# Stick-breaking attention layer on one core: output projection on six PSUM banks, with the FFN norm's transposes, copies and first gate matmuls reordered

## The reference, cut to what matters

```python
def rmsnorm(x, g):
    return x * lax.rsqrt(jnp.mean(x * x, axis=-1, keepdims=True) + RMS_EPS) * g
...
hn = rmsnorm(x, ln_mix_pre[i])
mixed = stick_breaking_mixer(hn, sb_w_qkv[j], sb_w_o[j])   # ends in o @ w_o
x = x + rmsnorm(mixed, ln_mix_post[i])
hn = rmsnorm(x, ln_ffn_pre[i])
x = x + rmsnorm(swiglu_ffn(hn, ffn_w_gu[i], ffn_w_down[i]), ln_ffn_post[i])
```

## Time and profile before

| | us |
|---|---|
| three timed runs | 1458.83, 1458.40, 1454.26 (median 1458.4) |
| the profiled execution, its own time | 1454.86 |
| its span, from first to last instruction | 1453.1 |
| around the span | 1.76 |
| TensorE matmuls busy | 1381.3 (95%) |
| VectorE, ScalarE, GpSimd busy | 697.4, 533.7, 379.9 |
| mean granted TensorE clock | 0.98 of full |

### The profile page before, as it was taken

How to read it: one execution, slowest core, us unless ns; L and a number is a source line. 1 busy time by engine, 2 the same in 40 slices (tenths; PEclk the granted TensorE clock), 3 DMA queues, 4 the chain that set the end, 5 groups by cost and what they waited for, 6 DMA issues and landing times.

```text
span 1453.1 us, 18360 instructions
## 1 busy us (share of the span) xinstructions
PE 1381.3 (95%) x6848; PEld 1153.4 (79%) x6848; DVE 697.4 (48%) x850; ACT 533.7 (37%) x948; POOL 379.9 (26%) x244
## 2 busy tenths in 40 slices
PE   5999999999999986997899999999999999999995
PEld 4788888888888875786688888888888888888884
DVE  6578788787887888232312222313031322223138
ACT  5566666666666664233122111111212121111113
POOL 4111011011011033263053233232413232332326
PEclk9999999999999988998899999999999999999998
DMA  4000000000000013020011111110102111111102
GB/s 188 30 30 21 25 30 30 15 29 29 15 29 29 15 52 123 30 73 29 15 58 59 44 44 43 43 58 29 67 20 72 43 58 43 43 43 43 58 14 117
DMA packets 18336, 66.66 MB, mean 46 GB/s; under 512 B 2032, under 2 KB 2032, under 8 KB 18288
## 3 DMA queue, kind: packets, MB, share of 16 engines
q1 hardware_dynamic: 16560, 59.78, 11.8%
q10 hardware_dynamic: 1728, 6.29, 1.3%
HBM read 61.87 MB, written 4.19 MB: 45 GB/s over the span
## 4 chain that ended last, share of the span: by engine, by line
PE 91%; DVE 6%; ACT 1%; DMA 1%; POOL 0%; issue 0%; POOLq 0%; ACTq 0%; DVEq 0%
PE bank L1134 11%; PE bank L1133 11%; PE bank L1135 11%; PE bank L980 6%; PE bank L982 6%; PE bank L981 6%; PE bank L1181 5%; PE bank L1180 5%; PE bank L1182 5%; PE bank L1084 4%; PE bank L1059 2%; PE bank L1058 2%; PE bank L1056 2%; PE bank L1104 2%; PE bank L1103 2%; PE bank L1029 2%
## 5 line engine op out<-in xcount | busy, mean ns | idle before, releaser
L681 POOL TENSOR_TENSOR w_lo<-raw,w_hi 128x1024 fp32r<-128x1024 f32 x89 | 216.7, 2439 | 770.4 <-ACT w_hi L421 770.2
L1133 PE MATMUL bank<-hnT_hi,w_hi 128*128 128x512 f32 x704 | 277.3, 394 | 2.9 <-DVE hnT_lo L782 2.9
L1134 PE MATMUL bank<-hnT_lo,w_hi 128*128 128x512 f32 x704 | 278.5, 396 | 0.0
L1135 PE MATMUL bank<-hnT_hi,w_lo 128*128 128x512 f32 x704 | 276.0, 392 | 0.0
L421 ACT ACTIVATE w_hi<-raw 128x1024 fp32r<-128x1024 f32 x89 | 93.4, 1060 | 404.6 <-PE bank L1135 353.4
L913 DVE TENSOR_TENSOR sg<-bank,sg 128x512 f32<-128x512 f32 x44 | 30.4, 692 | 437.7 <-ACT sg L614 437.7
L856 DVE TENSOR_TENSOR_SCAN stay<-stay,diag_one 128x256 f32<-128x256 f32 (+7 forms) x128 | 196.2, 1533 | 3.8 <-ACT stay L541 3.8
L927 DVE TENSOR_TENSOR y<-bank,y 128x512 f32<-128x512 f32 x176 | 119.3, 690 | 94.4 <-PE bank L1182 93.1
L1133 PEld LDWEIGHTS bank<-hnT_hi,w_hi 128*128 128x128 f32 x704 | 132.8, 189 | 34.7 <-DVE hnT_lo L782 3.5
L1135 PEld LDWEIGHTS bank<-hnT_hi,w_lo 128*128 128x128 f32 x704 | 132.9, 189 | 29.9
L429 ACT ACTIVATE AT_hi<-bank 128x512 fp32r<-128x512 f32 (+1 forms) x160 | 89.0, 556 | 183.2 <-PE bank L1084 182.5
(11 more groups left out here) (100 smaller groups left out, 2134.4 us busy)
## 6 DMA issues: line engine op xcount, KB each, us to landing
raw<-in_units SPq DMA_DIRECT2D x98, 512.0 KB, 3.3
acc<-in_x SPq DMA_DIRECT2D x8, 512.0 KB, 8.7
x_in<-in_x ACTq DMA_DIRECT2D x8, 512.0 KB, 3.4
out<-y SPq DMA_DIRECT2D x7, 512.0 KB, 2.6
g_pre_s<-in_mix_pre ACTq DMA_DIRECT2D x1, 512.0 KB, 5.5
g_post_t<-in_mix_post ACTq DMA_DIRECT2D x1, 512.0 KB, 4.2
g_ffn_t<-in_ffn_pre ACTq DMA_DIRECT2D x1, 512.0 KB, 3.7
g_out<-in_ffn_post ACTq DMA_DIRECT2D x1, 512.0 KB, 3.7
```

The source lines that it names most:

```text
L681: nc.gpsimd.tensor_tensor(w_lo[slot], raw[:, raw_slot, :], w_hi[slot].bitcast(F32), ALU.subtract).then_inc(w_ready, 1)
L1133: nc.tensor.matmul(bank_ap, wh, hnT_hi[:, kt, cols], start=(kt == 0), stop=False)
L1134: nc.tensor.matmul(bank_ap, wh, hnT_lo[:, kt, cols], start=False, stop=False)
L1135: mm = nc.tensor.matmul(bank_ap, wl, hnT_hi[:, kt, cols], start=False, stop=(kt == KT - 1))
```

## The change

Six mixed banks instead of four (`OB` added). The wait for the FFN's gain gets a semaphore of its own and moves behind the first scaling. On ScalarE the high part of tile t + 2 is copied between the squares of the two halves; on VectorE its low part comes ahead of the scaling. Norm tiles 0 and 1 are transposed before the last projection tile, tiles 1 and 3 into `OB`; their copies come first after it. The first gate runs in two halves of 256 columns. The transposes 4, 5 and 6 with 7 stand behind the groups (0,0), (2,0) and (1,0), and on VectorE hn(4) and hn(5) are made before the last scaling, hn(6) behind it, hn(7) after the low parts of tile 6.

```diff
--- before.py
+++ after.py
@@ -304,14 +304,20 @@
 FIRST_ACC_B = ACCB + OB
 GATEB, UPB = ZB, OB
 YB = ACCB + TB
-MIXB = ACCB + ZB
-FIRST_GATE_B = [ZB[0], ACCB[0], ZB[1], ACCB[1]]
+MIXB = ACCB + ZB + OB
+FIRST_GATE_B = [ACCB[0], ZB[0], ACCB[1], ZB[1]]
 ...
+def norm_bank(n):
+    if n < T_TRANS:
+        return TB[n % 2]
+    return (OB if (n - T_TRANS) // 2 in (1, 3) else TB)[n % 2]
 ...
@@ -337,6 +343,7 @@
 raw_in = [sem("raw_in0"), sem("raw_in1")]
 gain_in = sem("gain_in")
 gain2_in = sem("gain2_in")
+gain_ffn_in = sem("gain_ffn_in")
 gain3_in = sem("gain3_in")
 x_again = [sem("x_again0"), sem("x_again1")]
 out_done = sem("out_done")
@@ -578,30 +585,51 @@
     split_at(0, [])
     step(PAIRS, 0, proj=False, slots=TAIL_SLOTS)
     act.wait_ge(av_done, Z_ALL)
-    act.dma_start(g_ffn_t[:, :], g_ffn_pre.partition_broadcast(P)).then_inc(gain2_in, 16)
-    for t in range(NT):
-        for c in range(2):
-            act.wait_ge(mix_full, 2 * t + c + 1)
-            act.wait_ge(sq_done, square_index("mix", t, c))
-            nc.scalar.activation(junk_t[:, 0:HALF], MIXB[(2 * t + c) % 4][:, :], ACT.Square,
-                                 accum_out=ss_mix[:, 2 * t + c:2 * t + c + 1]).then_inc(sq_done, 1)
-        if t + 2 < NT:
-            o_hi_copy(t + 2)
+    act.dma_start(g_ffn_t[:, :], g_ffn_pre.partition_broadcast(P)).then_inc(gain_ffn_in, 16)
+    def mix_square(t, c):
+        act.wait_ge(mix_full, 2 * t + c + 1)
+        act.wait_ge(sq_done, square_index("mix", t, c))
+        nc.scalar.activation(junk_t[:, 0:HALF], MIXB[(2 * t + c) % 6][:, :], ACT.Square,
+                             accum_out=ss_mix[:, 2 * t + c:2 * t + c + 1]).then_inc(sq_done, 1)
+    def x2_square(t):
         act.wait_ge(x2_ready, t + 1)
         if t + 2 < NT:
             act.dma_start(x_in[:, t % 2, :], x_tiles[:, t + 2, :]).then_inc(x_again[t % 2], 16)
         act.wait_ge(sq_done, square_index("x2", t))
         nc.scalar.activation(blocks(junk_t[:, :]), x2(t), ACT.Square,
                              accum_out=ss[:, 2 * NT + t:2 * NT + t + 1]).then_inc(sq_done, 1)
-        if t in (1, 2):
-            split_at(t, [(t_full, T_TRANS)])
-    for t in range(NT):
+    def norm_hi(t):
         for half in range(2):
             n = T_TRANS + 2 * t + half
             t_hi_copy(n, hnT_hi[:, 4 * half:4 * half + 4, t * P:(t + 1) * P],
-                      TB[n % 2][:, :].rearrange("p (k c) -> p k c", k=4))
+                      norm_bank(n)[:, :].rearrange("p (k c) -> p k c", k=4))
+    for t in range(NT - 1):
+        mix_square(t, 0)
+        if t + 2 < NT:
+            o_hi_copy(t + 2)
+        mix_square(t, 1)
+        x2_square(t)
+        if t in (1, 2):
+            split_at(t, [(t_full, T_TRANS)])
+    act.wait_ge(mix_full, 2 * NT)
+    norm_hi(0)
+    norm_hi(1)
+    for c in range(2):
+        mix_square(NT - 1, c)
+    for t in (2, 3, 4):
+        norm_hi(t)
+    x2_square(NT - 1)
+    for t in (5, 6, 7):
+        norm_hi(t)
     act.dma_start(g_out[:, :], g_ffn_post.partition_broadcast(P)).then_inc(gain3_in, 16)
     def ffn_chunk(g, e, par, c):
@@ -783,7 +811,7 @@
     def norm_lo(index, t, half):
         ks, cols = slice(4 * half, 4 * half + 4), slice(t * P, (t + 1) * P)
-        t_lo_sub(index, hnT_lo[:, ks, cols], TB[index % 2][:, :].rearrange("p (k c) -> p k c", k=4),
+        t_lo_sub(index, hnT_lo[:, ks, cols], norm_bank(index)[:, :].rearrange("p (k c) -> p k c", k=4),
                  hnT_hi[:, ks, cols])
@@ -880,31 +908,39 @@
                                        in1=blocks(g_ffn_t[:, :]), op0=ALU.mult,
                                        op1=ALU.mult).then_inc(hn_ready, 1)
-    dve.wait_ge(gain2_in, 32)
-    for t in range(NT):
+    dve.wait_ge(gain2_in, 16)
+    def mix_scale(t):
         dve.wait_ge(rstd_done, NT + 2 * t + 1)
         for c in range(2):
-            nc.vector.scalar_tensor_tensor(out=x2(t, c), in0=blocks(MIXB[(2 * t + c) % 4][:, :]),
+            nc.vector.scalar_tensor_tensor(out=x2(t, c), in0=blocks(MIXB[(2 * t + c) % 6][:, :]),
                                            scalar=rstd[:, NT + t:NT + t + 1],
                                            in1=blocks(g_post_t[:, c * HALF:(c + 1) * HALF]),
                                            op0=ALU.mult, op1=ALU.mult).then_inc(mix_scaled, 1)
+    def norm_tile(t):
+        for half in range(2):
+            norm_lo(T_TRANS + 2 * t + half, t, half)
+    for t in range(NT - 1):
         if t + 2 < NT:
             o_lo_sub(t + 2)
+        mix_scale(t)
+        if t == 0:
+            dve.wait_ge(gain_ffn_in, 16)
         if t < RING:
             hn(t)
-    def norm_tile(t):
-        for half in range(2):
-            norm_lo(T_TRANS + 2 * t + half, t, half)
-    for t in range(RING):
+    hn(4)
+    hn(5)
+    for t in range(4):
         norm_tile(t)
-    for t in range(RING, NT, 2):
-        hn(t)
-        hn(t + 1)
+    mix_scale(NT - 1)
+    hn(6)
+    for t in (4, 5, 6):
         norm_tile(t)
-        norm_tile(t + 1)
+    hn(7)
+    norm_tile(7)
     def ffn_chunk(g, e, par, c):
         n = 4 * g + 2 * e + c
@@ -1021,9 +1057,9 @@
         if c == 0 and j == 0:
             pe.wait_ge(o_lo, t + 1)
-        if j == 0 and 2 * t + c >= 4:
-            pe.wait_ge(mix_scaled, 2 * t + c - 3)
-        dst = MIXB[(2 * t + c) % 4][:, :]
+        if j == 0 and 2 * t + c >= 6:
+            pe.wait_ge(mix_scaled, 2 * t + c - 5)
+        dst = MIXB[(2 * t + c) % 6][:, :]
         cols = slice(c * HALF, (c + 1) * HALF)
         oh, ol = o_hi_t[:, t % 2, j, :], o_lo_t[:, t % 2, j, :]
         nc.tensor.matmul(dst, oh, hnT_hi[:, j, cols], start=(j == 0), stop=False)
@@ -1119,20 +1155,31 @@
     step(PAIRS - 1, 1, proj=False)
     step(PAIRS, 0, proj=False, slots=TAIL_SLOTS)
-    for t in range(2, NT):
+    def out_project(t):
         for c in range(2):
             for j in range(PAIRS):
                 wo_part(t, c, j)
-    def gate_up(is_up, c, slot, bank_ap):
-        cols = slice(c * HALF, (c + 1) * HALF)
-        for kt in range(KT):
-            wh = w_hi[slot][:, kt * P:(kt + 1) * P]
-            wl = w_lo[slot][:, kt * P:(kt + 1) * P]
-            nc.tensor.matmul(bank_ap, wh, hnT_hi[:, kt, cols], start=(kt == 0), stop=False)
-            nc.tensor.matmul(bank_ap, wh, hnT_lo[:, kt, cols], start=False, stop=False)
-            mm = nc.tensor.matmul(bank_ap, wl, hnT_hi[:, kt, cols], start=False, stop=(kt == KT - 1))
+    def gate_up(is_up, c, slot, bank_ap, halves=1):
+        w = HALF // halves
+        for b in range(halves):
+            if halves > 1:
+                pe.wait_ge(t_lo, T_TRANS + 4 * (b + 1))
+            cols = slice(c * HALF + b * w, c * HALF + (b + 1) * w)
+            dst = bank_ap[:, b * w:(b + 1) * w]
+            for kt in range(KT):
+                wh = w_hi[slot][:, kt * P:(kt + 1) * P]
+                wl = w_lo[slot][:, kt * P:(kt + 1) * P]
+                last = b == halves - 1 and kt == KT - 1
+                nc.tensor.matmul(dst, wh, hnT_hi[:, kt, cols], start=(kt == 0 and b == 0), stop=False,
+                                 skip_group_check=halves > 1)
+                nc.tensor.matmul(dst, wh, hnT_lo[:, kt, cols], start=False, stop=False,
+                                 skip_group_check=halves > 1)
+                mm = nc.tensor.matmul(dst, wl, hnT_hi[:, kt, cols], start=False, stop=last,
+                                      skip_group_check=halves > 1)
         mm.then_inc(up_full if is_up else gate_full, 1)
     def gate_up_first(m, c):
@@ -1144,24 +1191,41 @@
             dst = UPB[c]
             if m == 3:
                 pe.wait_ge(prod_ready, c + 1)
-        gate_up(m % 2 == 1, c, ring(m), dst[:, :])
+        gate_up(m % 2 == 1, c, ring(m), dst[:, :], 2 if (m, c) == (0, 0) else 1)
     def norm_transpose(t):
         pe.wait_ge(hn_ready, NT + t + 1)
+        if t == 1:
+            pe.wait_ge(mix_scaled, 12)
+        else:
+            free = {0: -1, 2: 0, 3: 1, 4: 2, 5: 4, 6: 5, 7: 6}[t]
+            pe.wait_ge(t_lo, T_TRANS + 2 * free + 2)
         for half in range(2):
-            transpose_norm(T_TRANS + 2 * t + half, hn_t[:, t % RING, :], half)
-    for t in range(RING):
-        norm_transpose(t)
-    pe.wait_ge(t_lo, T_TRANS + 2 * RING)
-    pe.wait_ge(mix_scaled, 2 * NT)
-    for t, m in ((RING, 0), (RING + 2, 2)):
-        gate_up_first(m, 0)
-        norm_transpose(t)
-        norm_transpose(t + 1)
+            n = T_TRANS + 2 * t + half
+            for q in range(4):
+                k = 4 * half + q
+                mm = nc.tensor.transpose(norm_bank(n)[:, q * P:(q + 1) * P],
+                                         hn_t[:, t % RING, k * P:(k + 1) * P], ident[:, :])
+            mm.then_inc(t_full, 1)
+    for t in range(2, NT - 1):
+        out_project(t)
+    norm_transpose(0)
+    norm_transpose(1)
+    out_project(NT - 1)
+    norm_transpose(2)
+    norm_transpose(3)
+    pe.wait_ge(mix_scaled, 14)
+    gate_up_first(0, 0)
+    norm_transpose(4)
+    gate_up_first(2, 0)
```

(32 more changed lines are left out.)

## The result

The changed kernel takes 1440.53 us (median of 1440.13, 1440.51, 1440.54 and 1442.73), the kernel before 1457.42 (four runs, 1454.26 to 1458.83): ratio 0.989, 95% interval 0.9873 to 0.9906. The forecast was 1441.1. The profiled execution took 1440.54 us, with a span of 1438.7; before it was 1454.86 and 1453.1, so profile against profile 14.3 us are gained. One of the ten executions of experiment 1 took 1743.45 us at a granted clock of 0.75 and is left out of that experiment's ratio.

What follows compares the result with a forecast made beforehand. TensorE, busy for 95% of the span, was taken as the bound, so time comes only from its idle or low-clock stretches. 4.35 + 13.1 - 2.0 = 15.5 us off 1456.6 gives 1441.1 us; range 1436.8 to 1448.

Steps and rivals of the forecast that it cites:

- The first gap: TensorE's wait before projection tile 2: starts 2.95 us earlier, plus 1.4 us from no low clock, sum 4.35.
- A: Distance from tile 1's last matmul to tile 2's start: forecast 2.95 us gained.
- B: Distance from tile 2's start to tile 7's end: 1.4 us gained by full clock, 1.8 us of transposes added.
- the six banks are worth nothing by themselves: Projection's mixed banks: with four, no wait for a bank shows in the stretch, so no gain counted.
- Tiles 3 to 7: Projection tiles behind the first gap: little to spare at tile 5, low parts 1.2 us, but no stall.
- The tail: From tile 7's end to group (0,1): 44.4 us before, 29.5 after, 1.8 spent earlier, 13.1 us gained.
- C: Distance from tile 7's end to the start of group (0,1): forecast 29.5 us, before 44.4.
- the early transposes 0 and 1: Ahead of projection tile 7: cost 1.8 us on TensorE's path at full speed, their new wait nothing.
- The clock: Low clock expected in (0,1) after idle at transposes 6 and 7, costing 2.0 us; none at tile 7's end.
- D: Distance from (0,1)'s start to the span's end: forecast 2.0 us lost to the lower clock in (0,1).
- rival 1: Clock falls at tile 7's end too, price 1.5 to 3.5 us: gain 11.6 to 14.5, some 1443.5; chance 0.25.
- Rival 5: Clock falls at tile 7's end and stays low until (0,1): slower, 1460.5 us; chance 0.03.

Runs made afterwards that it cites:

- experiment 1: Kernel before with only the first gap's repair (early high and low parts, gain wait moved), four banks, old tail: 1455.99 us against 1456.83, ratio 0.9991.
- experiment 2: Kernel before with the first gap's repair and six mixed banks, old tail: 1451.45 us against 1456.34, ratio 0.9975.
- experiment 3: Changed kernel with four mixed banks again instead of six: 1445.78 us.
- experiment 4: Changed kernel with the low part of tile t + 2 behind the scaling of tile t on VectorE: 1448.98 us.
- experiment 5: Changed kernel with tile 7's chain ahead of the first norm copies on ScalarE and VectorE, TensorE's order untouched: 1449.45 us.
- experiment 6: Changed kernel with the first gate as one group of 24 matmuls of 512 columns: 1444.31 us.
- experiment 7: Changed kernel with transposes 0 and 1 behind the last projection tile, hn(4) and hn(5) behind the low parts of tiles 0 to 3: 1440.67 us.
- experiment 9: Changed kernel with twelve unread filler matmuls, eight between transposes 6 and 7 and four behind transposes 7: 1438.94 us.
- experiment 10: Changed kernel with hn(7) ahead of tile 6's low parts and transposes 5 to 7 interleaved with the gate groups: 1437.6 us, ratio to before 0.9866.

## Why the prediction was right

**The first gap: right in size, wrong in one reason.** Forecast 2.95 us of start time; measured 2.86 (A). The low clock behind it was to give 1.4; B without the transposes is 68.64 - (69.40 - 1.66) = 0.9 shorter, 0.24 of the rest is a new wait at tile 5, and the first matmul behind each of three stops took 0.1 longer. The step that failed is "the six banks are worth nothing by themselves: with four, no wait for a bank shows in the stretch". A wait that ends earlier than another at the same instruction shows in no trace. Experiments 1 to 3 put its price at 1.8 us of A (2.98 and 2.96 against 1.13 and 1.12), and up to 1.4 more where the clock falls. The size came out right because the change had the banks, which by the prediction's own reasoning is luck. The code showed it: tile 2's half 0 waits for one scaling, and my own account had the scaling of tile 0 starting behind the low part. The load of the gain, which the prediction named as what held the scaling, cost 0.6 us at most by the rows, and taking it away gained nothing in experiment 4.

**Tiles 3 to 7: right but for 0.24 us.** There is one wait, before tile 5 (638.22 instead of 637.98). It was announced as the narrowest place, but with a low part of 1.2 us. VectorE's, TensorE's and GpSimd's timelines of the changed kernel:

```profile
635.09 3.08 DVE L860 TENSOR_TENSOR o_lo_t<-acc,o_hi_t 128x1024 fp32r<-128x1024 f32 x1 [0.27 <-ACT o_hi_t L510]
...
638.22 0.50 PE L1065 MATMUL bank<-hnT_hi,o_hi_t 128*128 128x512 f32 x1
```

```profile
613.06 1.11 POOL L749 TENSOR_TENSOR ss<-ss_mix 128x1 f32<-128x1 f32 x1 [1.47 <-ACT junk_t L594]
```

The low part took 3.08 us, for the reason that the last section shows. GpSimd's adds of tiles 0 to 5 took the short time, 2.40, as forecast, but the chain gained nothing by it: the low part now runs beside the small sum ahead of the root (L749), which took 0.66 to 1.18 us in tiles 0 to 5 where it took 0.19 to 0.65 before. Tile 5's add starts 56.7 us behind tile 1's last matmul (659.90), in the kernel before 55.1 (658.61), although tile 2 starts 2.9 earlier; the second squares, now behind the early copies, come later too.

**The tail: right.** Forecast 29.5 us for C, measured 29.42: transposes 2 at 2.26 (2.3), the gate at 4.3 (4.4), the halves 0.12 apart and 0.2 more in all than I had, transposes in a running stream 0.8 instead of 0.9, transposes 7 3.8 behind transposes 6 (3.95). The covers were thinner than said, since the chain came late: tile 6's squares ended at 672.94, 0.7 us before tile 7 did (673.68) and not "some 3 us", and tile 5 was scaled 0.9 us before transposes 0 asked for it (659.8, 660.72), at the edge of "about 1 to 4". That nothing waited there is partly luck. Experiment 5 shows the mechanism: with tile 7's chain ahead of the copies, and nothing else changed, 7.7 us of the sum return (4.8 by medians). Halving the gate is worth 3.75 (experiment 6), 2.4 for the start and 1.3 for the rest, the clock less what whole matmuls save. What the prediction counted as the price of a useful step, the early transposes 0 and 1, is not useful: the same tail with them late is 1.3 us shorter (experiment 7). The sum had the price right (1.66 for 1.8) and never asked what the tail would be without it.

**The clock: right in place, undersized.** Forecast a fall at the last transposes for 2.0 us within 1.4 to 2.7; measured 2.74 (experiment 9). D took 0.35 more than that, which stays open. At tile 7's end I expected none, and the changed kernel's two profiles have none. But of the eight profiles in which TensorE stands still there for 2.10 us, two show it (experiments 3 and 10), at a price of 1.5 and 1.3 us up to transposes 4, where 1.5 to 3.5 was forecast. So rival 1 is real, and that it didn't come in the changed kernel's profile is luck in part; two of eight are too few to weigh its chance of 0.25. Rival 5 (low clock throughout) needed the fall to last; in experiment 5, with 8.90 us of idle time the worst case, it was back before the first gate (whose matmuls stand 0.12 apart from 689.5 on).

**The sum.** 15.5 us forecast, 14.0 by the distances. The failed terms are small and of both signs: A 0.1 less, B 0.35 less, C 0.1 more, D 1.1 less. (Rival 1's lower end is 11.3 by the prediction's own prices, 17.5 - 2.7 - 3.5, and not 11.6; the range was widened past it anyway.) Against the medians it is 16.9 us in the first series and 11.8 in the second. So the 0.6 us between forecast and median is closer than the runs can tell. The spread for which the forecast was set against the mean of four executions, 4 us, is real. Part of it comes ahead of the stretch: where the granted clock of the first 60 us was 1.00, tile 1's last matmul started at 602.6 to 603.6 us (seven profiles), and where it was 0.95 to 0.97, at 604.7 to 607.2 (seven); the rest of the difference between the two series stays open.

## What to carry to other kernels

When a wait is removed, list every other condition on the same instruction and work out when each is met: the trace shows only the last, and here a repair that shortened the distances by 3.5 us together with its second part (experiment 2) shortened them by 0.1 without it (experiment 1). Put the copies that the next stage needs ahead of a reduction chain that it needs later, and place work so that each producer's latency (here 2.6 us for a tile) is covered by at least as long a run of matmuls behind it. Filling a wait with work that has to be done anyway beat doing that work early, by 1.3 us here (experiment 7). Compare variants by distances inside the trace when the timed runs scatter by more than the effect, and remember that one trace is one execution: in two comparisons here distances and medians differed by 3 us.
